# Multiplying the first two weight tiles behind two norms with x before it is normed, in a two-block transformer kernel on one core

## What is computed

```python
def rms_norm_2(x, g):
    xf = x.astype(jnp.float32)
    y = xf * lax.rsqrt(jnp.mean(xf * xf, axis=-1, keepdims=True) + EPS)
    return (y * g.astype(jnp.float32)).astype(x.dtype)
...
    return rms_norm(x) * final_norm          # end of the first block
...
    h = rms_norm_2(x, norm1_g)               # hybrid_layer
    z = h @ w_in + b_in                      # split into the inputs of four branches
...
    x = x + merged @ w_o
    h2 = rms_norm_2(x, norm2_g)
    x = x + jnp.square(jax.nn.relu(h2 @ w_up)) @ w_down
    return x
```

## Time and profile before

| | before |
|---|---|
| median of three runs | 3505.84 us (3501.34 to 3517.44) |
| the profiled execution | 3507.6 us, its span 3505.5 us |
| TensorE busy | 3451.8 us (98%) |
| VectorE, ScalarE, GpSimd busy | 1773.7, 1181.9, 269.8 us |
| granted TensorE clock, mean | 0.990 |
| DMA | 107 GB/s, queue busy 32% |

### The profile page before, as it was taken

One profiled execution on the slowest core, in us unless ns is written; L12 is line 12 of the kernel. 1 busy time (PEld: TensorE's weight loads), 2 busy tenths in 40 slices (PEclk: granted clock), 3 DMA queues, 4 the chain that ended last, 5 costly groups with the idle time before them and its releaser, 6 DMA issues.

```text
span 3505.5 us, 40940 instructions
## 1 busy us (share of the span) xinstructions
PE 3451.8 (98%) x16724; PEld 2753.1 (79%) x16724; DVE 1773.7 (51%) x3070; ACT 1181.9 (34%) x1986; POOL 269.8 (8%) x226
## 2 busy tenths in 40 slices
PE   9999999999999999999999999999999999999999
PEld 7888786777888788878777888887688777878887
DVE  7666456565666733334655543334453665454433
ACT  3222236543222322223555232224222444223322
POOL 0000211002000200021100200022011000020000
PEclk9999999999999999999999999999999999999999
DMA  6555321123565523232210322322222223122232
GB/s 242 205 210 189 107 92 59 43 77 111 195 219 192 183 92 104 93 103 94 69 55 26 114 90 90 102 84 84 64 81 68 69 69 119 38 95 88 97 104 78
DMA packets 120217, 376.36 MB, mean 107 GB/s; under 512 B 13280, under 2 KB 28000, under 8 KB 120032
## 3 DMA queue, kind: packets, MB, share of 16 engines
q1 hardware_dynamic: 120032, 373.76, 32.3%
HBM read 371.61 MB, written 2.10 MB: 107 GB/s over the span
## 4 chain that ended last, share of the span: by engine, by line
PE 93%; DVE 4%; ACT 2%; issue 0%; POOL 0%; DMA 0%; SPq 0%; ACTq 0%; DVEq 0%; POOLq 0%
PE ps L445 26%; PE ps L447 26%; PE ps L446 26%; PE ps L666 2%; PE ps L689 2%; PE ps L561 2%; PE ps L488 1%; PE ps L479 1%; PE ps L481 1%; PE ps L480 1%; PE ps L495 1%; DVE s_wl L1447 1%; PE ps L500 1%; ACT s_wh L956 0%; PE ps L528 0%
## 5 line engine op out<-in xcount | busy, mean ns | idle before, releaser
L445 PE MATMUL ps<-s_uh,s_wh 128*128 128x512 f32 x2824 | 1131.3, 401 | 21.6 <-ACT s_sg L1196 10.5
L1447 DVE TENSOR_TENSOR s_wl<-s_raw,s_wh 128x1024 fp32r<-128x1024 f32 (+3 forms) x645 | 708.1, 1099 | 847.1 <-ACT s_wh L956 845.5
L447 PE MATMUL ps<-s_ul,s_wh 128*128 128x512 f32 x2824 | 1106.4, 392 | 0.0
L446 PE MATMUL ps<-s_uh,s_wl 128*128 128x512 f32 x2824 | 1106.0, 392 | 0.0
L956 ACT ACTIVATE s_wh<-s_raw 128x1024 fp32r<-128x1024 f32 (+3 forms) x645 | 588.1, 913 | 738.1 <-PE ps L447 549.6
L445 PEld LDWEIGHTS ps<-s_uh,s_wh 128*128 128x128 f32 x2824 | 534.4, 189 | 167.4 <-issue 41.9
L447 PEld LDWEIGHTS ps<-s_ul,s_wh 128*128 128x128 f32 x2824 | 533.5, 189 | 113.6
L446 PEld LDWEIGHTS ps<-s_uh,s_wl 128*128 128x128 f32 x2824 | 534.4, 189 | 107.8 <-issue 2.4
L447 PE MATMUL ps<-s_fl,s_wh 128*128 128x512 f32 x960 | 378.2, 394 | 0.0
L445 PE MATMUL ps<-s_fh,s_wh 128*128 128x512 f32 x960 | 378.2, 394 | 0.0
L446 PE MATMUL ps<-s_fh,s_wl 128*128 128x512 f32 x960 | 378.2, 394 | 0.0
(11 more groups left out here) (405 smaller groups left out, 3377.0 us busy)
## 6 DMA issues: line engine op xcount, KB each, us to landing
s_raw<-w SPq DMA_DIRECT2D x616, 512.0 KB, 3.6
s_raw<-w SPq DMA_DIRECT2D x96, 192.0 KB, 2.3
s_raw<-w SPq DMA_DIRECT2D x64, 256.0 KB, 2.6
s_raw<-w SPq DMA_DIRECT2D x19, 128.0 KB, 2.0
s_x<-x SPq DMA_DIRECT2D x4, 512.0 KB, 6.5
out<-s_x SPq DMA_DIRECT2D x8, 256.0 KB, 2.4
s_raw<-w SPq DMA_DIRECT2D x4, 420.0 KB, 4.3
s_crow<-crow SPq DMA_DIRECT2D x2, 512.0 KB, 4.5
```

Of the source, the lines that this page charges most:

```text
L445: TE.matmul(o, w_hi(i, k), h, start=first, stop=False)
L446: TE.matmul(o, w_lo(i, k), h, start=False, stop=False)
L447: return TE.matmul(o, w_hi(i, k), l, start=False, stop=last)
L1447: V.tensor_tensor(wl[w][:, 0:n], raw[t % NRAW][:, 0:n], wh[w][:, 0:n].bitcast(F32), SUB).then_inc(*s_lo.up(("lo", t)))
```

## The change

The first two tiles behind each of the two norms are multiplied with x times gain, not yet normed. `gained` makes the halves `gxh` and `gxl` of that product, slice by slice, in the last steps of the FFN `f21` and of `wo2`. `raw_pair` is a pair over these halves; inside it stand the norm's sums and rows. The results get the row's factor afterwards: in the branch block ACT copies them to `lqk` and DVE multiplies them there with the row's bank; in the FFN ACT writes the ReLU to `acc` and `more`, and DVE multiplies it with the row's bank. Tiles 2 and 3 now make a normal pair. Their `get` on ACT and DVE stands in the middle of `apply` (`two_pairs`), and so do the copies of the raw results of the branch block (`raw_copies`). The keep-warm matmuls of the norm "up" are gone. The order of tiles in `plan()` follows; the weights and their number stay.

```diff
+        def raw_pair(st, g0, g1, name, between):
+            i0, i1 = get(name, 0, 0), get(name, 0, 128)
+            o0, o1 = take(g0), take(g1)
+            for k in range(8):
+                between.get(k, lambda: None)()
+                pe.wait_ge(*s_dve["gx", st, k])
+                a = three(o0[:, :], i0, k, gxh[:, k, :], gxl[:, k, :], k == 0, k == 7)
+                b = three(o1[:, :], i1, k, gxh[:, k, :], gxl[:, k, :], k == 0, k == 7)
+            a.then_inc(*s_pe.up(("w", i0), ("ps", g0)))
+            b.then_inc(*s_pe.up(("w", i1), ("ps", g1)))
+        def norm_sums(st, parts):
+            for j, (ap, wait) in enumerate(parts):
+                o = take(("ms", st, j))
+                pe.wait_ge(*wait)
+                sums(o, 0, ap).then_inc(*s_pe.up(("ps", ("ms", st, j))))
...
-                    if jj == 0:
-                        fm_pair(("g", st, 0), g, 0, ("u", st, 0) if u else ("g", st, 1), u or g, 0 if u else 1, ("u", st))
-                    elif u or jj > 1:
+                    if jj == 0 and not u:
+                        raw_pair(st, ("g", st, 0), ("g", st, 1), g, {2: lambda: norm_sums(st, tail(st)), 4: lambda: row(("r", st), tmp[2], True)})
+                    elif jj == 0:
+                        fm_pair(("g", st, 0), g, 0, ("u", st, 0), u, 0, ("u", st))
+                    elif jj == 2 and not u:
+                        fm_pair(("g", st, 2), g, 2, ("g", st, 3), g, 3, ("u", st))
+                    elif u or jj > 3:
                         fm(("g", st, jj), g, 8, jj, uh, ul, ("u", st))
...
         def second():
             u = ("u", "s")
+            raw_pair("s", ("ml", 0), ("ml", 1), "zml", {2: final_sums, 6: final_rows})
             ring[:] = [list(range(6)), (bank_of["r", "s"] + 1) % 8 % 6]
             pe.wait_ge(*SEL)
-            fm_pair(("ml", 0), "zml", 0, ("ml", 1), "zml", 1, u)
-            for i in range(2, 13):
+            fm_pair(("ml", 2), "zml", 2, ("ml", 3), "zml", 3, u)
+            for i in range(4, 13):
                 fm(("ml", i), "zml", 8, i, uh, ul, u)
...
         second()
-        norm("up", tail("up"), tmp[2])
         ffn("up")
...
+        def two_pairs(name, then=None):
+            def at(k):
+                if k == 1:
+                    fm_pair(name, 0, name, 1)
+                if k == 2:
+                    get(name, 0, 256, 1)
+                    get(name, 0, 384, 0)
+                if k == 4 and then:
+                    then()
+            return at
...
+        def gained(st, m, gain):
+            SC.activation(gxh[:, m, :], x[:, m, :], ACT.Identity, bias=0.0, scale=gain(m)).then_inc(*s_act.up(("gx", st, m)))
...
         def second():
-            act.wait_ge(*s_dve["bgh"])
-            fm_pair("zml", 0, "zml", 1)
-            for i in range(8):
-                if i > 1:
+            for i in range(2):
+                act.wait_ge(*s_dve["ml", i])
+                SC.activation(lqk[:, i, :], lqk[:, i, :], ACT.Identity, bias=col("bml", i)).then_inc(*s_act.up(("lqk", i)))
+            for i in range(2, 8):
+                if i > 3:
                     fm("zml", 8, i)
                 act.wait_ge(*s_pe["ps", ("ml", i)])
...
+        def raw_copies():
+            for i in range(2):
+                copy(("ml", i), lqk[:, i, :], bank(("ml", i))[:], ("ml raw", i))
+
+        apply("s", 8, uh, None, two_pairs("zml", raw_copies))
...
+        apply("up", 8, uh, None, two_pairs("up2"))
...
+        def gained(st, m, gain):
+            dve.wait_ge(*s_act["gx", st, m])
+            V.scalar_tensor_tensor(gxl[:, m, :], x[:, m, :], gain(m), gxh[:, m, :].bitcast(F32), MUL, SUB).then_inc(*s_dve.up(("gx", st, m)))
...
-                    elif (u or jj > 1) and not (first and jj < 4):
+                    elif (u or jj > 3) and not (first and jj < 4):
                         fm(g, 8, jj, 0, st)
...
                         dve.wait_ge(*s_act["gate", st, jj])
+                        if jj < 2:
+                            V.tensor_tensor(s[:], s[:], bank(("r", st))[:], MUL).then_inc(*s_dve.up(("normed", st, jj), frees=("r", st) if jj else None))
+                            dve.wait_ge(*s_dve["normed", st, jj])
                         V.tensor_tensor(s[:], s[:], s[:], MUL).then_inc(*s_dve.up(("prod", st, jj)))
...
+        for i in range(2):
+            dve.wait_ge(*s_act["ml raw", i])
+            V.tensor_tensor(lqk[:, i, :], lqk[:, i, :], bank(("r", "s"))[:], MUL).then_inc(*s_dve.up(("ml", i), frees=("r", "s") if i else None))
```

More of the change, by code:

```diff
@@ L36, in ffn @@
                     pair(g, 0, u, 0)
-                elif j < 2 and not u:
-                    if j == 0:
-                        pair(g, 0, g, 1)
+                elif j < 4 and not u:
+                    if j % 2 == 0:
+                        pair(g, j, g, j + 1)
                 else:
@@ L105, in plan @@
     pair("zml", 0, "zml", 1)
-    for c in range(2, 13):
+    pair("zml", 2, "zml", 3)
+    for c in range(4, 13):
         fm("zml", 8, c)
@@ L318, in program @@
         with ExitStack() as d:
+            gxh, gxl = sb(d, "gxh", [128, 8, 512], F32R), sb(d, "gxl", [128, 8, 512], F32R)
+        with ExitStack() as d:
             lqk = sb(d, "lqk", [128, 8, 512])
@@ L702, in mix, with final_sums, final_rows @@
             s_pe.mark(("end", st))
+        def final_sums():
+            o = take(("fs", 0))
+            pe.wait_ge(*s_pool["sq", "s"])
+            sums(o, 0, acc)
+            pe.wait_ge(*s_pool["sq fin"])
+            sums(o, 4, more).then_inc(*s_pe.up(("ps", ("fs", 0))))
+            o = take(("fs", 1))
+            pe.wait_ge(*s_act["tail", "s"])
+            sums(o, 0, tmp[1]).then_inc(*s_pe.up(("ps", ("fs", 1))))
+            o = take(("fs", 2))
+            pe.wait_ge(*s_act["tail fin"])
+            sums(o, 0, tmp[3]).then_inc(*s_pe.up(("ps", ("fs", 2))))
+        def final_rows():
+            row(("r1",), tmp[2])
+            row(("r", "s"), tmp[0])
         def gate(c, b):
@@ L1014, in ffn @@
                     jj = a0 + j
-                    s = tmp[jj % 4]
-                    if jj == 0 and not first:
-                        fm_pair(g, 0, u or g, 0 if u else 1)
-                    elif (u or jj > 1) and not (first and jj < 4):
+                    s = tmp[jj % 4] if u or jj > 1 else (acc, more)[jj]
+                    if jj == 0 and u and not first:
+                        fm_pair(g, 0, u, 0)
+                    elif (u or jj > 3) and not (first and jj < 4):
                         fm(g, 8, jj, 0, st)
@@ L1396, in second @@
                 fm("wo2", 8, m)
+                if m < 7:
+                    act.wait_ge(*s_dve["x", "up", m])
+                    gained("up", m, lambda k: col("n2", k))
             square("up", 7, tmp[1])
+            gained("up", 7, lambda k: col("n2", k))
             barrier("s")
@@ L1518, in apply @@
                     V.scalar_tensor_tensor(tmp[k % 4][:], src[:, k, :], scale(k), more[:] if after_k and k else bank(g)[:], MUL, MUL).then_inc(
-                        *s_dve.up(("ap", st, k), frees=g if k == (0 if after_k else n - 1) else None))
+                        *s_dve.up(("ap", st, k), frees=g if last and k == (0 if after_k else n - 1) else None))
                     if after_k:
@@ L1563, in ffn @@
                     update(("d", st, a0, m), m, gate, ("x", after if a0 + n == nf else (st, a0), m))
+                    if st == "f21" and a0 + n == nf:
+                        for k in (m - 1,) if m < 7 else (6, 7):
+                            if k >= 0:
+                                gained("s", k, lambda k: small[:, 64 + k:65 + k])
             while tiles.side:
@@ L1840, in second @@
             V.tensor_scalar(bgh[:], col("bg", 0, 32), 0.5, None, MUL).then_inc(*s_dve.up("bgh"))
-            fm_pair("zml", 0, "zml", 1)
-            for i in range(2, 9):
+            for i in range(4, 9):
                 fm("zml", 8, i)
@@ L2048, in second @@
                 update(("wo", "s", m), m, None, ("x", "up", m))
+                for k in (m - 1,) if m < 7 else (6, 7):
+                    if k >= 0:
+                        gained("up", k, lambda k: col("n2", k))
             barrier("s")
```

17 lines of the change are left out of this document (11 added, 6 removed).

## The result

| | before | after |
|---|---|---|
| median of six runs each | 3504.01 us (3501.34 to 3517.44) | 3526.93 us (3523.68 to 3532.82) |
| the profiled execution, its span | 3507.6, 3505.5 us | 3525.95, 3524.1 us |
| TensorE's mean granted clock | 0.990 | 0.987 |

A forecast was written before the change was run, and what follows sets the result against it. TensorE bounds the kernel (busy 3451.8 of 3505.5 us), so only its idle or half-clock stretches can move the time. First norm +13.1 and second +7.5 sum to +20.6 us: 3526 beside the median, range 3515 to 3533.

The forecast's parts named there:

- Raw pair at 0.5 us behind the FFN, gained copies free: First norm: raw pair waits only for its weights, starting about 0.5 us behind the FFN; gained copies cost nothing.
- The rival of late copies: Gained copies are late, so the raw pair starts after the sums' inputs; up to 3 us more, 3529; chance 0.03.
- The sums bring the clock down: First norm, inside the raw pair: 32 sums take 4.0 us and the clock falls, a restart costing 2.84 us.
- The rival in which the clock holds through the sums: First norm: no clock fall in the sums, or quicker recovery in one restart; 3.5 us less, 3523; chance 0.17.
- R: Moment the norm's row result is ready and DVE can start applying it; forecast 2399.5 at the first norm.
- Bank 4 ends the wait before the second pair: First norm: second pair waits for ACT's copy of the raw result in bank 4, R + 10.6, after 8.1 us idle.
- Tile 4 waits for ACT's reads and scalings: First norm: tile 4's split waits behind two result reads and four scalings, starting at P (second pair's end) + 6.45.
- The split beside POOL's products: First norm, tile 4: DVE's split takes 2.18 instead of 1.23 us beside POOL's products, 0.95 more.
- Each cold restart at 2.84 us: Both norms: each restart of TensorE at the lower clock level costs 2.84 us over full pace.
- "up", waits: Second norm: 2.1 us idle before the second pair, 8.4 us before tile 4.
- The rival of a further fall there: Second norm: without keep-warm matmuls, sums and row bring the clock down; +2.84, 3529; chance 0.12.
- The side on which it could have been no change: Both norms: tile 4's split is not late, removing its idle and two restarts; -20.5, 3506; chance 0.06.

The follow-up runs named there:

- after_again: The changed kernel, nothing altered, profiled a second time for one execution; first stretch 96.3, middle 671.3, second stretch 75.0 us.
- a2_bank: Changed kernel with the first norm's sums in banks 0 to 2, rows in 6 and 7, the ring of six starting at 0; 3521.39 us, ratio 1.0047.
- a1_split4: Changed kernel with the split of tile 4 moved inside `apply`, ahead of slice 6 and of ACT's reads of results; 3508.56 us, ratio 1.0011.
- b4_finer: b1_reads_later with a2_bank's banks, first raw tile finished earlier, tile 2 split before `apply`, tile 4 behind it, sums of "s" in two parts; 3494.56 us, ratio 0.9974.
- b3_gaps_warm: Changed kernel with keep-warm matmuls in its four gaps, 7 and 5 calls at "s", 1 and 7 at "up"; 3525.65 us, ratio 1.0053.
- b1_reads_later: a1_split4 with tile 4's own request called ahead of result 2, so tile 5 is split before results 2 and 3 are read; 3507.72 us, ratio 1.0015.
- a3_first_only: Changed kernel with the change kept at norm "s" only, norm "up" and the last FFN as before; 3516.77 us, ratio 1.0038.

## Why the prediction was right

It put the loss in the right places, by the right causes, at sizes somewhat too large at both norms, and that the total came out within a microsecond is in part luck: a difference that it did not foresee made up for them. By its own steps:

- **Raw pair at 0.5 us behind the FFN, gained copies free: right.** It started 0.57 us behind the end, after 0.41 idle. The rival of late copies is out.
- **The sums bring the clock down: right, but at half the price.** They took 3.65 us where 4.0 was taken over from the head norm, the rows 1.71 where 2.0 was. In the raw pair 7 matmuls were slow (2385.96 to 2389.08), 1.5 us more than at full pace, not 2.84. The rival in which the clock holds through the sums is out: in after_again it fell there too, with 8 slow matmuls. R came 15.5 us after the raw pair's start; 17.2 was forecast.
- **Bank 4 ends the wait before the second pair: right.** DVE started `apply` at 2394.97, and the pair came 10.55 us later; 10.6 was forecast. Idle 7.82 for 8.1. a2_bank shows that it was the bank.
- **Tile 4 waits for ACT's reads and scalings: right.** The second pair took 12.86 us, to P = 2418.38, and the tile began at P + 5.9 for P + 6.45. ACT's timeline of the changed kernel shows the queue as it was counted, two reads and four scalings ahead of the rounding:

```profile
2417.89 0.69 ACT L1305 ACTIVATE s_lqk<-ps,s_cst 128x512 f32<-128x512 f32 x1 [5.38 <-PE ps L450]
2418.48 1.32 ACT L1295 ACTIVATE s_x<-s_x,s_cst 128x512 f32<-128x512 f32 x2
2419.70 0.67 ACT L1305 ACTIVATE s_lqk<-ps,s_cst 128x512 f32<-128x512 f32 x1
2420.27 1.33 ACT L1295 ACTIVATE s_x<-s_x,s_cst 128x512 f32<-128x512 f32 x2
2421.50 2.94 ACT L985 ACTIVATE s_wh<-s_raw 128x1024 fp32r<-128x1024 f32 x3
```

- **The split beside POOL's products: too dear.** 0.95 us was taken from a single row. DVE began tile 4's split at 2422.58 and TensorE the tile at 2424.28, 1.70 us later; at "up", where POOL is silent, the same step took 1.28 (3186.01 to 3187.29). The difference of 0.42 lies in the 0 to 1.27 that the Trainium skill's rule of an exclusive lock allowed (SBUF — State Buffer, "SBUF: two separate sides"); a range as wide as that does not test the rule. DVE's three splits and POOL's four products at "s", from the changed kernel's timelines:

```profile
2422.58 4.90 DVE L1505 TENSOR_TENSOR s_wl<-s_raw,s_wh 128x1024 fp32r<-128x1024 f32 x3 [10.75 <-ACT s_wh L985]
...
2419.33 5.93 POOL L2274 TENSOR_TENSOR s_x<-s_x,s_acc 128x512 f32<-128x512 f32 x4 [30.16 <-ACT s_x L1295]
```

and DVE's three splits at "up":

```profile
3186.01 3.50 DVE L1505 TENSOR_TENSOR s_wl<-s_raw,s_wh 128x1024 fp32r<-128x1024 f32 x3 [0.25 <-ACT s_wh L985]
```

  The three take 4.90 us beside POOL's work and 3.50 without it.
- **Each cold restart at 2.84 us: the term of the sum that was mis-sized.** The restarts of the first norm cost 1.5 (7 slow matmuls, records of over 0.5 us), 2.0 (9) and 2.7 us (13), that of the second 1.9 (9); the stretches at the low clock were 3.1, 4.0, 5.7 and 4.0 us, where four of 5.6 were forecast. With the one restart that before has in any case, +9.9 was measured for +13.1 at the first norm and +6.5 for +7.5 at the second: 2.3 us of the first difference and 0.9 of the second are the restarts'. A price from one row was used four times as if it were fixed.
- **"up", waits: right to 0.1 to 0.4 us.** From the raw pair's start at 3152.39 to the second pair 15.71 us (15.7 forecast), to tile 4 34.90 (35.0); the idle times 1.82 for 2.1 and 8.05 for 8.4. ACT's timeline of the changed kernel has the four ReLUs of results 0 to 3 ahead of the rounding of tile 4, which begins 2.35 us before the tile:

```profile
3175.53 0.58 ACT L1067 ACTIVATE s_acc<-ps 128x512 f32<-128x512 f32 x1
...
3182.95 0.58 ACT L1067 ACTIVATE s_tmp<-ps 128x512 f32<-128x512 f32 x1
...
3184.94 2.94 ACT L985 ACTIVATE s_wh<-s_raw 128x1024 fp32r<-128x1024 f32 x3
```

  The rival of a further fall there is out: the window from the raw pair to the wait before tile 4, of the changed kernel, is all at full clock:

```profile
3152.40:3179.20 26.80, 24.98 (x121) 20.43 (x119) 17.74 (x29) 10.55 (x17) 1.02 (x1) 1.00 0.18 60
```

- **The side on which it could have been no change: out.** It was worth 20.5 us by the prediction; a1_split4, which builds it, gave 18 in the medians and 13.0 in the stretches, since smaller waits came up behind.
- **The sum.** The stretches give +16.4 where +20.6 was forecast, and the medians +22.9. The two profiles differ by 18.6. Against the second pair of profiles it is 96.3 + 75.0 less 85.0 + 68.4, +17.9. The interval of the medians' difference is 16.5 to 28.0 us. So 3 to 4 us of the forecast's agreement with the median are chance: restarts sized too large stood in for a difference of the medians that the stretches do not hold, and that these runs do not explain.

## What to carry to other kernels

Work that is moved out of a norm's shadow leaves the lookahead of the other engines' lists where it stood: before a wait on TensorE is filled, list what ACT and DVE will have queued ahead of the next weights' split and who still has to read each bank of the ring. The change lost 22.9 us with that order wrong; with the splits, the reads and the banks in a better order (b4_finer) it gained 8.2. And compare stretches of two executions of each kernel before a few us are given a cause.

## What the runs showed of the hardware

The price of a cold restart is not a constant. In one execution of the changed kernel it was 7, 9, 13 and 9 slow matmuls behind waits of 0, 7.8, 5.7 and 8.1 us: the longest wait had not the dearest restart, and the first came with no wait at all, behind 32 records of one column. Nor does a wait set its price: the one of 5.75 us had 13 slow matmuls in one execution and 6 in the other. Two of these waits end warm when matmuls without use fill them to their last 1.81 and 1.47 us (b3_gaps_warm), the third, filled to its last 2.04 us, does not.

From execution to execution of one kernel, the low clock falls on the same stage at different lengths. In the 40 us from 3000 on, the changed kernel had a granted clock of 0.80 and 0.95 in its two executions; its middle came out at 676.4 and 671.3 us with no edit between. a2_bank, b3_gaps_warm and b1_reads_later had 681.9 to 684.2 us in a middle that the rest of the table has at 671 to 676. The traces show where they lie. Between the same two instructions of the middle, some 220 matmuls apart, TensorE is busy all the time in every run. Seven of the twelve executions take 40.0 to 40.2 us there at a granted clock of 0.87. The others take 43.3 (a3_first_only, 0.80), 44.6 (after, 0.77), 50.6 (b1_reads_later, 0.66), 53.5 (b3_gaps_warm, 0.62) and 53.6 us (a2_bank, 0.62). The windows of after_again, after and a2_bank:

```profile
3010.04:3050.07 40.03, 40.03 (x222) 33.72 (x222) 10.01 (x26) 7.18 (x10) 9.15 (x8) 0.87 0.07 21
...
3010.65:3055.20 44.55, 44.55 (x221) 37.09 (x221) 10.62 (x26) 7.18 (x10) 8.08 (x8) 0.77 0.07 19
...
3006.00:3059.57 53.57, 53.57 (x222) 44.18 (x222) 10.29 (x25) 7.18 (x10) 8.08 (x8) 0.62 0.05 15
```

So what these middles have over 671 us is the same work at the low clock, in one place. Whether an edit made it likelier stays open: each of these kernels had one execution in the profiler, and nothing of their edits lies there. For a2_bank it is not the rule, since that execution, 3530.16 us, was the slowest of its six, and the others took 3518.3 to 3522.9. The experiments ran on three chips, and that of the first two profiles is not on record, so a part of what differs between two executions of one kernel may be the chip's; a2_bank's six were on one.
